# A transformer kernel on one core: the order of a block's rest, its product and the norm's root

## What is computed

```python
h = rmsnorm(x, mix_norm[layer])                          # layer 0: windowed attention, layer 1: RG-LRU
x = x + mixer(h) @ w_out
h = rmsnorm(x, ffn_norm[layer])
u = causal_dwconv(h @ w_up, conv_w, conv_b)              # 3 taps over tokens
g, v = split(u)
x = x + (gelu(g) * v) @ w_down                           # d_ff = 3 * 2048
...
h = h + mixed_attention(rms_norm(h)) * silu(gate) @ w_out_even
h = h + dilated_attention(rms_norm(h)) * silu(gate) @ w_out_odd
return rms_norm(h, final_norm_g)
```

## Time and profile before

| | |
|---|---|
| median of 3 runs | 3245.12 us (3237.54 to 3246.34) |
| the profiled execution's own time | 3241.82 us |
| its span, first to last instruction | 3240.0 us |
| PE busy | 3139.2 us, 97% |
| PE weight loads busy | 2782.8 us, 86% |
| VectorE busy | 2320.9 us, 72% |
| ACT busy | 1655.4 us, 51% |
| DMA engines, mean share of the main queue | 49.0% |
| mean granted clock of the tensor engine | 0.990 |

### The profile page before, as it was taken

The page is one execution under the profiler, slowest core; times in us unless marked ns, Lnnn a source line. Parts: engine busy times, 40 slices in busy tenths (PEclk is TensorE's granted clock), DMA queues, the critical chain, the costliest instruction groups (busy, mean ns, idle before and its releaser), DMA issues.

```text
span 3240.0 us, 52960 instructions
## 1 busy us (share of the span) xinstructions
PE 3139.2 (97%) x18904; PEld 2782.8 (86%) x18904; DVE 2320.9 (72%) x3626; ACT 1655.4 (51%) x2188; POOL 13.5 (0%) x20
## 2 busy tenths in 40 slices
PE   8999999999999999899999999999899999999987
PEld 7988888888888899788888888888798888888876
DVE  6877885786687777778767866877576666666665
ACT  5664554554455466645545544554445654444443
POOL 1000000000000000000000000000000000000000
PEclk9999999999999999999999999999999999999998
DMA  5335555555555444455555555555434445454443
GB/s 206 121 119 179 196 193 182 191 185 186 190 189 187 163 173 166 153 180 193 189 187 187 189 183 193 185 186 194 161 125 162 156 156 182 156 180 168 168 154 119
DMA packets 83066, 561.50 MB, mean 173 GB/s; under 512 B 9729, under 2 KB 12801, under 8 KB 15873
## 3 DMA queue, kind: packets, MB, share of 16 engines
q1 hardware_dynamic: 82944, 559.87, 49.0%
HBM read 557.73 MB, written 2.10 MB: 173 GB/s over the span
## 4 chain that ended last, share of the span: by engine, by line
PE 73%; DVE 11%; DMA 8%; ACT 4%; issue 4%; DVEq 1%; SPq 0%; ACTq 0%
PE unit L278 42%; PE unit L281 22%; DVE w_tail L1187 5%; ACT w_head L803 2%; DMA raw<-in_even_b 1%; DMA raw<-in_lru_out 1%; PE unit L493 1%; DMA raw<-in_lru_y 1%; DMA raw<-in_even_out 1%; DMA raw<-in_lru_x 1%; PE unit L495 1%; PE unit L494 1%; DMA raw<-in_wo 1%; DVE prod L1193 1%; ACT lo L810 1%
## 5 line engine op out<-in xcount | busy, mean ns | idle before, releaser
L803 ACT ACTIVATE w_head<-raw 128x2048 fp32r<-128x2048 f32 (+1 forms) x540 | 1013.8, 1877 | 643.1 <-DMA raw<-in_up 200.8
L1187 DVE TENSOR_TENSOR w_tail<-raw,w_head 128x2048 fp32r<-128x2048 f32 (+1 forms) x540 | 1209.7, 2240 | 50.2 <-ACT w_head L803 40.4
L278 PE MATMUL unit<-h,w_head 128*128 128x512 f32 x4912 | 1197.6, 392 | 3.1 <-DVE h L1210 2.7
L278 PEld LDWEIGHTS unit<-h,w_head 128*128 128x128 f32 x4912 | 904.1, 189 | 180.6 <-DVE h L1210 4.0
L281 PE MATMUL unit<-h,w_tail 128*128 128x256 f32 x4912 | 669.4, 285 | 0.0
L281 PEld LDWEIGHTS unit<-h,w_tail 128*128 128x128 f32 x4912 | 637.5, 192 | 22.4 <-issue 2.7
L278 PE MATMUL unit<-act,w_head 128*128 128x512 f32 x2464 | 607.0, 394 | 12.0 <-DVE prod L1193 6.4
L1193 DVE TENSOR_TENSOR prod<-unit,lo 128x256 f32<-128x256 f32 x468 | 198.3, 424 | 586.6 <-ACT lo L810 583.4
L278 PEld LDWEIGHTS unit<-act,w_head 128*128 128x128 f32 x2464 | 455.7, 189 | 106.4 <-DVE act L1204 7.4
L281 PE MATMUL unit<-act,w_tail 128*128 128x256 f32 x2464 | 337.0, 283 | 0.0
L281 PEld LDWEIGHTS unit<-act,w_tail 128*128 128x128 f32 x2464 | 323.4, 191 | 11.6
(11 more groups left out here) (250 smaller groups left out, 2240.1 us busy)
## 6 DMA issues: line engine op xcount, KB each, us to landing
raw<-in_up SPq DMA_DIRECT2D x192, 1024.0 KB, 4.8
raw<-in_down SPq DMA_DIRECT2D x96, 1024.0 KB, 4.8
raw<-in_odd SPq DMA_DIRECT2D x64, 1024.0 KB, 4.8
raw<-in_even_b SPq DMA_DIRECT2D x32, 1024.0 KB, 4.8
raw<-in_attn SPq DMA_DIRECT2D x24, 1024.0 KB, 4.9
raw<-in_wo SPq DMA_DIRECT2D x16, 1024.0 KB, 4.8
raw<-in_lru_x SPq DMA_DIRECT2D x16, 1024.0 KB, 4.8
raw<-in_lru_y SPq DMA_DIRECT2D x16, 1024.0 KB, 4.9
```

The costliest lines, as they stand in the source:

```text
L278: pe.matmul(bank[:, :], w_head[:, slot, k * P:(k + 1) * P], src[:, k, :], start=k == 0, stop=False)
L803: a.activation(w_head[:, slot, 0:width], raw[:, r, 0:width], ACT.Copy).then_inc(head_done, 1)
L1187: v.tensor_tensor(w_tail[:, slot, 0:width], raw[:, slot % 2, 0:width], w_head[:, slot, 0:width].bitcast(F32), ALU.subtract).then_inc(tail_ ...
```

## The change

It has three parts.

1. In `residual` on VectorE the rest of block m+3 is made first, ahead of block m's product, and not after the sum and the split.
2. Ahead of each norm whose stage follows (norms 1 to 5) the rounding and the rest of the new stage's block 3 are moved from behind the root to ahead of it: `stage_split` on ACT before it waits for the sum over the partitions, `stage_tail` on VectorE before it waits for the root. The first step of the stage leaves them out. In gates both stand around the small computation of lambda: the rounding ahead of ACT's exponential for it, the rest behind VectorE's last operation of it.
3. In the last block of each up stage the convolution, the gelu product and the split into `act` come ahead of the rest. For this the last group of four is written out and no longer part of the loop.

```diff
+            def stage_split(name):
+                split(BASE[name] + LEAD, LEAD)
...
             def up(name, layer, r):
                 def body(i):
                     for j in range(RING):
-                        step(i * RING + (BASE[name] + j), j)
+                        step(i * RING + (BASE[name] + j), j, r == 0 and known(i) and i == 0 and j == 0)
...
             def ffn(layer, norm):
+                stage_split(f"up{layer}0")
                 token_norm(norm)
...
+            stage_split("lru")
             token_norm(2)
...
-            lru_split(0, 3)
             for i in range(LRU_BLOCKS):
...
+            stage_split("gates")
             a.wait_ge(lam_in, 1)
             a.activation(lamb[:, 2:4], lamb[:, 0:2], ACT.Exp).then_inc(lam_done, 1)
             token_norm(4)
...
-                step(BASE["gates"] + j, j)
+                step(BASE["gates"] + j, j, j == 0)
...
-                        step(u + j, j)
+                        step(u + j, j, not trail and j == 0)
...
+            stage_split("odd")
             token_norm(5)
...
+            def stage_tail(name):
+                tail(BASE[name] + LEAD, LEAD)
...
                 def body(i, last=False):
                     for j in range(RING):
                         u, m = i * RING + (BASE[name] + j), i * RING + j
+                        if not last or j == 0:
+                            tail(u + LEAD, j + LEAD)
                         product(u, j)
                         add = v.tensor_tensor(x[:, m, :], x[:, m, :], prod[:, :], ALU.add)
...
-                        if not last or j == 0:
-                            tail(u + LEAD, j + LEAD)
                         if final:
                             accumulate(m + KT * (norm - 1), known(m) and m == 0)
...
-                def body(i):
+                def body(i, final=False):
                     for j in range(RING):
                         u, c = i * RING + (BASE[name] + j), i * RING + (CONVS[name] + j)
+                        last = final and j == RING - 1
                         product(u, j)
                         scaled(kv[:, 0, :]).then_inc(conv_in, 1)
-                        tail(u + LEAD, j + LEAD)
+                        if not last and not (r == 0 and known(i) and i == 0 and j == 0):
+                            tail(u + LEAD, j + LEAD)
...
                             split_act(i * 2 + j // 2, kv[:, 6, :]).then_inc(act_done, 1)
-                repeat(v, 0, 32 // RING, body, chain)
+                        if last:
+                            tail(u + LEAD, j + LEAD)
+                repeat(v, 0, 32 // RING - 1, body, chain)
+                body(32 // RING - 1, True)
...
             def ffn(layer, norm):
+                stage_tail(f"up{layer}0")
                 token_norm(norm)
...
+            stage_tail("lru")
             token_norm(2)
...
-            lru_tail(0, 3)
...
+            stage_tail("gates")
             token_norm(4)
...
-                tail(BASE["gates"] + j + LEAD, j + LEAD)
+                if j:
+                    tail(BASE["gates"] + j + LEAD, j + LEAD)
...
-                        tail(u + j + LEAD, j + LEAD)
+                        if trail or j:
+                            tail(u + j + LEAD, j + LEAD)
...
+            stage_tail("odd")
             token_norm(5)
```

## The result

| | before | changed |
|---|---|---|
| median | 3244.44 us, 4 runs (3237.54 to 3246.34) | 3222.07 us, 4 runs (3218.26 to 3224.75) |
| ratio | | 0.9934 [0.9918, 0.995] |
| the profiled execution's own time | 3241.82 us | 3222.52 us |
| its span | 3240.0 us | 3220.4 us |

The change saves 22.4 us by the medians, 19.3 us between the two profiled executions. I had forecast a gain of 12.2, a time of 3233 and a range whose low end was 3224.

What follows compares the result with a forecast made beforehand. The prediction took PE, 97% busy, as the bound, with a 5.65 us loop setting the stages with a norm. Terms -8.7 - 3.7 + 0.2 = -12.2 us gave 3229.6 on the profiled execution, 3233 by the median; range 3224 to 3248.

Steps and rivals of the forecast that it cites:

- The closed loop: Stages with a norm: product, sum, square, rounding, rest in turn set 5.65 us a block, 5.40 in the first blocks.
- Products 0: Each stage's first product, now behind block 3's rest: lru_out at 1368.45, even_out 0.6 later, wo's rest fits in idle time.
- two loads 2.2 us apart would share the engines: Rival, down stages: loads of blocks 4 and 5 share the engines; sum +2, 3247 us; chance 0.07.
- Part 3: Up stages' ends: PE's 0.89 wait for `act` goes; -3.7 for four, its gain in down02 and down12 within their -0.5 each.
- The step that failed: Opening step, whole kernel: PE is 97% busy, so only what shortens its idle time counts.
- the 1.92 for `acc`: At wo's norm: PE's 1.92 us for the rest and `acc` goes, as `acc` is ready 0.4 behind h.
- the first four stretches: Stretches up to the sums of norms 1 to 4: forecast gains 3.4, 2.35, 1.0 and 2.35 us.
- The fifth: Stretch from norm 4's sum to norm 5's, gates to even_out: forecast gain 3.1 us.
- The sixth stretch: Stretch from norm 5's sum to the last norm's, odd and odd_out: forecast gain 0.
- PE's pace: Rival, stages with a norm: loop hops shrink, period at or under 5.57; gain 17 to 19, 3227 us; chance 0.15.
- The waits did change their name: Rival, norms: waits gone at `acc` return at h, period 5.72 to 5.85, gain 0 to 8; chance 0.18.
- Longer hops in the loop: Rival, loop through the square: period over 5.85 makes the kernel slower, at 5.95 3251 us; chance 0.10.

Runs made afterwards that it cites:

- The one more operation: Changed kernel with the square's sum into `acc` moved from behind the split into h to between rest and next product: 3250.08 us, 1.0012 of before.
- the opened loop: Changed kernel with ACT's square behind the next block's rounding and its sum into `acc` behind that block's rest on VectorE: 3213.6 us, 0.9902 of before.
- part 1 alone: Kernel before with only the rest of block m+3 put ahead of product m in residual: 3224.31 us, 0.9939 of before.
- part 3 alone: Kernel before with only the last up block's convolution, gelu product and split put ahead of the rest: 3243.45 us, 0.9995 of before.

## Why the prediction was right in kind and short in size

**The closed loop held.** Forecast 5.65 in it and 5.40 ahead of it. The changed kernel shows 5.38 ahead of it, and in it 5.58 and 5.71 at a turn in wo, 5.61 to 5.66 and 5.81 in lru_out: 5.60 and 5.66 a block. The excess of 0.20 for a turn was read about right (0.13 to 0.20). What the sum had wrong is that four steps and not three go at 5.38; in wo products 0 and 15 stand at 225.82 and 308.97, 83.15 apart against 84.0. With the end of the stage (in wo 2.66 from product 15 to the sum, forecast 2.82) product 0 to norm is 85.8 against 86.8 forecast in wo, 86.6 in lru_out and 86.35 in even_out. The one more operation and the opened loop, 25 and 11 to the two sides, show that this loop sets the pace.

**Products 0.** lru_out's stands 4.16 behind its rounding (forecast 4.2):

```profile
1355.72 1.91 ACT L803 ACTIVATE w_head<-raw 128x2048 fp32r<-128x2048 f32 x1
...
1357.67 2.29 DVE L1193 TENSOR_TENSOR w_tail<-raw,w_head 128x2048 fp32r<-128x2048 f32 x1 [3.01 <-ACT w_head L803]
1359.88 0.42 DVE L1202 TENSOR_TENSOR prod<-unit,lo 128x256 f32<-128x256 f32 x1
1360.44 0.76 PE L278 MATMUL unit<-act,w_head 128*128 128x512 f32 x1 [4.33 <-DVE prod L1202]
```

That PE waits 4.33 for it (2.4 was the longest such wait before) is the price of this order, which I had counted in the start of the stage. down02's step of 7.03 is the 7.00 worked out. That two loads 2.2 us apart would share the engines did not happen: the step has room for one load of 4.74 and no more.

**Part 3.** At each of the four boundaries it brings 1.10 (forecast 0.9), read as the shift between the down stage before and the one after. But in front of a norm I should have given it below zero: the experiment without it there is 3.8 less, while my sum had 0.5 for the stage with part 3's gain in it, and never asked what the stage would do without part 3. Alone it brought 1.4 by the medians, part 1 alone 20.8, all three 20.5: they do not add up. In part this is the loss ahead of a norm, in part the clock, as told below.

**The step that failed** is the first one, "only what shortens its idle time counts", and with it the price of a wait: the 1.92 for `acc` went into the sum as 1.92, and what the tensor engine's clock loses behind such a wait was put at nothing. PE's busy time itself fell, from 3139.2 to 3132.3 us (3136.4 in the second trace of the changed kernel). By an estimate from the runs (below) this was about 4 us of the gain. The rest of what was missing, 5.4, lies in terms of the right mechanism that were sized too small: 4.4 in the first four stretches and 0.7 in even_out.

By the table of norms the first four stretches gave 13.5 where I had 9.1. Product 0 to norm was 1.0 shorter than forecast in wo and 0.2 in lru_out, each of the four boundaries without a norm gave 0.2 more, and the rest is down02 and down12, which I had at 0.5 each: they gained 1.4 to 1.9 with what follows to the next product 0.

The fifth gave 2.3 where I had 3.1: even_out itself gave 4.0, but the stages between norm 4 and even_out gave back 1.7. Here too the clock shows. The same piece of the program, in the kernel before and in the changed one (window, us, PE, PEld, DVE, ACT and POOL busy, granted clock, share of the DMA engines, GB/s):

```profile
2321.00:2351.00 30.00, 22.25 (x140) 20.79 (x141) 16.19 (x30) 8.64 (x12) 0.00 (x0) 0.89 0.31 108
2308.00:2338.00 30.00, 22.63 (x127) 21.19 (x128) 14.30 (x23) 8.73 (x12) 0.00 (x0) 0.83 0.30 106
```

The lower clock took 5.1 us of these 30 in the changed kernel and 3.3 in the one before. In the other traces the kernels that arrived there early gave back about 1 to 2, and the one with part 3 alone, which arrived as late as before and has no more of the lower clock there, next to nothing. The two go together but not one to one, so the clock is a part of it, and what else is, I have not tested.

The sixth stretch, 3.8, was no part of the forecast. 2.9 of it stand right behind norm 5. odd_out itself gave nothing, as forecast (products 0 and 15 are 83.49 and 83.54 apart). The 1.0 left comes ahead of its first product, most of it in the first matmuls of the stage, where the kernel before stayed longer at the lower clock:

```profile
3127.00:3132.00 5.00, 5.00 (x20) 4.22 (x19) 1.15 (x3) 1.96 (x2) 0.00 (x0) 0.65 0.00 0
3108.00:3113.00 5.00, 5.00 (x24) 4.28 (x23) 3.34 (x4) 2.12 (x2) 0.00 (x0) 0.82 0.00 0
```

**The clock behind a wait.** I had priced the 1.92 for `acc` as 1.92. In the kernel before, the norm's sum of norm 5 takes 1.22 where that of norm 1 takes 0.70: the tensor engine had been granted 1.2 GHz and not 2.4. The 30 us around it:

```profile
2720.00:2750.00 30.00, 27.07 (x134) 22.69 (x132) 18.59 (x24) 12.76 (x16) 0.00 (x0) 0.89 0.48 176
```

The same around norms 3, 4 and 5 of the changed kernel:

```profile
1442.00:1472.00 30.00, 30.00 (x170) 26.24 (x169) 25.07 (x39) 16.82 (x21) 0.00 (x0) 1.00 0.50 174
2247.00:2277.00 30.00, 28.07 (x157) 24.22 (x156) 22.32 (x37) 15.49 (x21) 0.00 (x0) 1.00 0.45 164
2705.00:2735.00 30.00, 28.22 (x160) 24.51 (x159) 19.99 (x26) 13.27 (x18) 0.00 (x0) 1.00 0.51 181
```

and of the kernel with part 3 alone, in which every norm shows it:

```profile
1452.00:1482.00 30.00, 26.88 (x144) 23.00 (x143) 23.82 (x37) 16.54 (x21) 0.00 (x0) 0.94 0.55 191
2260.00:2290.00 30.00, 26.63 (x142) 22.75 (x141) 21.09 (x35) 15.28 (x20) 0.00 (x0) 0.94 0.54 180
2722.00:2752.00 30.00, 27.18 (x147) 23.29 (x146) 19.74 (x25) 12.26 (x14) 0.00 (x0) 0.94 0.57 193
```

0.94 over 30 us is 1.8 us not had, 0.89 is 3.3. Over all traces, at norms 1 to 5: with the old order, where PE waits 1.9 for `acc` and mostly some more for h or a bank before it, 9 of 16 norms show such a stretch. With the new order PE waits once, 1.3 to 1.9, at 23 norms, and 5 of these show one, all five behind a wait of 1.8 or 1.9. At 11 norms of the new order and at the 15 of the opened loop it does not wait, and none of these 26 does. By the traces the old order lost 3.3, 8.4 and 9.0 us at its five norms, a mean of 6.9; the new one 0 to 1.8, a mean of 1.2.

The mean granted clock is known for every execution, and so gives a wider basis. What the clock is short of 1, times the span, is 35.7 us on average over the 45 executions of the kernel before, and 31.5 over nine of the changed one (0.9890 and 0.9902). These 4.2 us, give or take 2, are an estimate of the clock's part of a gain of 21.8 between the means (what of it falls into waits of PE costs nothing, so it is on the high side); the other 17.6 stand against the 12.2 of the forecast. Part 3 alone, with a stretch at all five norms, is at 38.3 over 11 executions, 2.3 worse than the kernel before in its group. Without the clock its gain would be 4.4, near the 4.7 that my forecast's working gives: the clock took most of it. It can also be why the profiled execution of before, with one such stretch only, lay 3.3 under its median.

The link between wait and clock rests on counts. The one norm that I put back into the old order had no such stretch in its trace, so it is shown as a frequency over many norms and not at a single one; I made no kernel that adds a wait and nothing else.

The Trainium skill (TensorE: Matmul & The Clock Gate, Part 1) says that a gate sets this clock by how busy PE has been of late, and that the same kernel can show it differently from run to run. The runs here agree with both: in all 14 traces the stretches at the lower clock come behind waits of PE only, and behind the norms two executions of the changed kernel show none and one.

**The rivals.** PE's pace came nearest in time (3227), by other terms than its own: the period did not reach 5.57. To be right by it would have been luck. The waits did change their name at four of five norms, but 1.9 became 1.3 to 1.8, and at the third nothing. Longer hops in the loop did not occur by themselves; added on purpose they cost 25, where the forecast's price gave 20. The chance of 0.57 for faster was too low by what I had left out.

## What to carry to other kernels

When an instruction moves ahead of another, write down the closed loop that it makes, hop by hop from start to start, and compare its period with the bound engine's; what stands inside that loop costs its full time even on engines that are half idle, and what can be taken out of it (here the square ahead of the rounding) can bring half as much again as the change that made the loop: 0.9902 of before against 0.9934. Price parts in the company in which they run, since one part can eat what another brings until the loop is open. And when a change takes away waits of the tensor engine near 2 us, look at the granted clock behind them over more than one execution: here it was worth some 4 us of 22, which the length of the waits does not contain.

## What the runs showed of the hardware

The tensor engine's lower clock came in stretches behind waits, and not each time. At the norms: 9 of 16 where PE waited 1.9 and mostly a little more before it, 3 of 5 where it waited 2.0 to 2.2 for h (the kernel with one more operation in the loop), 5 of 23 at 1.3 to 1.9, 0 of 26 where it did not wait. A stretch behind a norm cost 1.8 to 3.3 us. Of the 3.3 us between the spans of two executions of the changed kernel, 3220.4 and 3223.7, one such stretch is about half. A VectorE operation behind a rest recorded at 2.29 us started 2.20 to 2.21 behind its start in every kernel; the small operation recorded at 0.42 lengthened a chain by 0.33.
